# The first input projection as three rounded products, and the norms between products taken tile by tile

## The chip, the cores and the metric

The kernel runs on one core of one Trainium2 chip. The metric is the device time of one execution in microseconds. TensorE (PE) multiplies, and its weight loads are shown as an engine of their own (PEld). VectorE (DVE), ScalarE (ACT) and GpSimd (POOL) do the rest of the arithmetic, and SyncE (SP) issues the loads of the weights.

## The reference, cut to what matters

Two sequences of 256 tokens each, the latents and their context, of width 1024, go through a stack of layers. Every layer is a norm, a product with a weight matrix, a mixer of some kind (attention, mLSTM, RWKV, a gated feed-forward), and a product back that is added to the residual rows. All inputs and outputs are float32. What the change touches is this:

```
def rms_norm(x, eps=NORM_EPS):
    xf = x.astype(jnp.float32)
    return (xf * lax.rsqrt(jnp.mean(xf * xf, axis=-1, keepdims=True) + eps)).astype(x.dtype)

def modulate(x, shift, scale):
    return rms_norm(x) * (1.0 + scale) + shift

def ab_mixer(h_l, h_c, w_in, gate_b, q_norm, k_norm, ...):
    splits = [NA_WIDTH, 2 * NA_WIDTH, 3 * NA_WIDTH, 3 * NA_WIDTH + ML_WIDTH, ...]
    def project(h):
        qa, ka, va, qb, kb, vb, ob, g = jnp.split(h @ w_in, splits, axis=-1)
        qa = rms_norm(split_heads(qa, NA_HEADS, NA_HEAD_DIM)) * q_norm
        ka = rms_norm(split_heads(ka, NA_HEADS, NA_HEAD_DIM)) * k_norm
        ...
    qa_l, ka_l, va_l, qb_l, kb_l, vb_l, ob_l, g_l = project(h_l)
    qa_c, ka_c, va_c, qb_c, kb_c, vb_c, ob_c, g_c = project(h_c)
```

`w_in` is 1024 x 3600: seven parts of 512 columns and 16 columns of gates.

## The kernel before

Token rows lie in `x` (latents) and `cx` (context), each as two tiles of 128 tokens by 1024. A norm's result is wanted the other way round, as eight blocks of 128 features by 256 tokens, so every norm ends in 16 transposes on PE. Weights come in slabs of 1024 rows by 512 columns (2 MB) through a ring of three places. SP issues the load of a slab when PE has used the slab three before it.

There are two kinds of product. The first (`rows_pe`, line 557) multiplies float32 by float32. The profile records two matmuls for each one written, so the 224 matmuls of the first projection stand as 448. The second kind works with rounded parts (float32r): each operand is split into a rounded high part and a low part, which is what the rounding left, and three products high x high, high x low, low x high are summed (`rows3_pe` line 380, `mlp_pe` lines 1366 and 1381, the feed-forwards line 2249). There the high part of a slab is made by ACT (`high_act`, line 336, two halves of four blocks), the low part by DVE (`low_dve`, line 343), one or two slabs ahead of PE.

Each engine has its own program, written out in order at the end of `bidir_dual_stack`. Nothing is rearranged by a scheduler, so what stands behind a waiting instruction on its engine waits too. Semaphores tie the engines together through named events.

**The first projection.** `first_mod_dve` (line 532) applies scale and shift to the eight blocks `hT[:, k, :]` (512 tokens wide: latents and context together). `ab_in_pe` then runs seven slabs of four token tiles by eight blocks, in PSUM banks 0 to 3, and after that the four gate products of four columns each, `psum[0:4, 4 + g, :]` (line 763), each with all 512 tokens as moving operand. `ab_in_act` copies every finished tile out of PSUM (lines 776 to 782). `qk_norm_dve` takes squares of `qa` and `ka`, POOL the root, DVE multiplies (line 801), PE transposes (line 833), and DVE copies out of PSUM (line 812) before the neighbourhood attention starts (line 857). POOL meanwhile loads and masks the attention's bias table (`bias_pool`, line 633) ahead of these roots.

**The norms between products.** There are eleven places: L0m with C0m, L1a with C1a, L1m, pre0, mix0, xx0, post0, pre1, mix1, xx1, post1 (L: latents, C: context; the others latents). At each the chain is: DVE adds the product to the rows (line 2221, or 1340 and 1342 with a gate); when the last tile is added, ACT takes squares of both tiles (`norm_act`, line 408, 1024 wide); POOL makes the inverse root of both (`norm_pool`, lines 416 and 418); DVE multiplies both tiles (line 428, into `sc`); PE transposes, block by block and in it tile by tile (`norm_pe`, line 471), so nothing starts before tile 1 is there; DVE copies out. For a product in rounded parts that is, for each block, high and low: lines 449 and 452 without a shift, lines 441, 444 and 446 with one. Otherwise it is one instruction (lines 456, 458). The next product waits for pairs of blocks. In the DVE program the norm of L0m is done, then the low part of the next slab, then the norm of C0m, and only then does the first feed-forward (`mlp0`) start on PE:

```
            norm_pe(pe, "L0m")
            norm_pe(pe, "C0m")
            mlp_pe(pe, "mlp0", x_parts, (0, 1), "L0m")
```

## Time and profile before

| | |
|---|---|
| time, median of 3 runs | 3435.55 us (3427.95 to 3437.43) |
| the profiled execution | 3440.02 us, its span 3438.2 us, mean granted clock 0.941 |
| PE busy | 3122.3 us (91%) |
| PEld busy | 2324.8 us (68%) |
| DVE busy | 1697.6 us (49%) |
| ACT busy | 963.3 us (28%) |
| POOL busy | 282.4 us (8%) |
| read from HBM | 400.67 MB, 117 GB/s over the span |

Start and duration in a row of the timeline are microseconds from the span's start; "x16" counts instructions that were merged into the row, and the bracket gives idle time of the engine before it and what ended it. A matmul's recorded duration includes its way through the array, so successive matmuls overlap: the rate is read from the distance between starts.

### The profile page before, as it was taken

How to read it: one execution, taken by the hardware profiler on the slowest of the kernel's cores; microseconds unless marked ns; L12 is line 12 of the kernel's file. 1: busy time of each engine (PE TensorE's matmuls, PEld its weight loads, DVE VectorE, ACT ScalarE, POOL GpSimd, SP SyncE). 2: the span in 40 equal slices, each digit the busy share in tenths (PEclk: the TensorE clock that was granted, in tenths of full speed). 3: DMA queues.
4: the chain of work that ended last, by engine and by line, in shares of the span. 5: the costliest groups of instructions: out<-in, count | busy, mean ns of one | idle time of the engine just before them, and what ended most of it. 6: DMA issues, size and time to landing. Idle time of an engine off the chain costs nothing. (4 is left out here: it accounts for less than half of the span.)

```text
span 3438.2 us, 54550 instructions
## 1 busy us (share of the span) xinstructions
PE 3122.3 (91%) x24312; PEld 2324.8 (68%) x24312; DVE 1697.6 (49%) x2689; ACT 963.3 (28%) x1489; POOL 282.4 (8%) x362
## 2 busy tenths in 40 slices
PE   7999988799996977989978989999899999998899
PEld 2443333398994536888866979874579898455697
DVE  1104356465556108777755555455445453465453
ACT  1012310133331115443312333322223332142332
POOL 1202011000000012232310000000000000200000
PEclk9998989899998988999979999999999999999999
DMA  8311344245453210000024545542245554323253
GB/s 252 102 55 62 135 147 172 73 147 196 172 196 95 92 25 2 3 3 3 4 81 141 193 150 172 187 165 89 98 144 168 165 183 169 128 74 123 74 192 128
DMA packets 249827, 409.23 MB, mean 119 GB/s; under 512 B 10055, under 2 KB 102616, under 8 KB 249464
## 3 DMA queue, kind: packets, MB, share of 16 engines
q1 hardware_dynamic: 244824, 390.39, 33.3%
q0 software_dynamic: 4768, 15.35, 1.8%
q8 instruction: 191, 3.13, 0.4%
q14 instruction: 44, 0.36, 0.0%
HBM read 400.67 MB, written 2.95 MB: 117 GB/s over the span
## 5 line engine op out<-in xcount | busy, mean ns | idle before, releaser
L343 DVE TENSOR_TENSOR ring_parts<-ring,arena_parts 128x2048 fp32r<-128x2048 f32 x250 | 553.0, 2254 | 276.9 <-ACT arena_parts L336 274.6
L336 ACT CAST arena_parts<-ring 128x2048 fp32r<-128x2048 f32 x250 | 457.3, 1879 | 601.3 <-PE psum L2249 229.5
L2249 PE MATMUL psum<-arena_parts 128*128 128x256 f32 x2816 | 514.8, 286 | 6.4 <-DVE arena_parts L452 6.2
L2249 PEld LDWEIGHTS psum<-arena_parts 128*128 128x128 f32 x2816 | 444.0, 194 | 9.2 <-DVE arena_parts L452 9.2
L557 PE MATMUL psum<-ring,hT 128*128 128x512 f32 (+1 forms) x960 | 414.2, 593 | 9.1 <-DVE hT L1308 2.6
L2249 PE MATMUL psum<-arena_parts,ring_parts 128*128 128x256 f32 x1408 | 400.8, 285 | 0.0
L557 PEld LDWEIGHTS psum<-ring,hT 128*128 128x128 f32 x960 | 184.0, 192 | 234.5 <-issue 223.1
L380 PE MATMUL psum<-arena_parts 128*128 128x512 f32 x928 | 291.9, 396 | 8.3 <-DVE arena_parts L2285 8.1
L2249 PEld LDWEIGHTS psum<-arena_parts,ring_parts 128*128 128x128 f32 x1408 | 272.9, 194 | 0.0
L1381 PE MATMUL psum<-arena_parts 128*128 128x512 f32 x768 | 240.5, 395 | 7.8 <-DVE arena_parts L1428 7.8
L380 PEld LDWEIGHTS psum<-arena_parts 128*128 128x128 f32 x928 | 176.8, 191 | 46.6 <-DVE arena_parts L2285 9.0
L680 PE MATMUL psum<-ring,arena 128*24 128x512 f32 (+2 forms) x384 | 188.4, 625 | 3.1 <-DMA ring<-in_ada_w 3.1
L1366 PE MATMUL psum<-arena_parts 128*128 128x256 f32 x1024 | 187.9, 286 | 3.6 <-DVE arena_parts L446 3.6
L380 PE MATMUL psum<-ring_parts,arena_parts 128*128 128x512 f32 x464 | 182.6, 394 | 0.0
L1381 PEld LDWEIGHTS psum<-arena_parts 128*128 128x128 f32 x768 | 145.7, 191 | 38.5 <-DVE arena_parts L1428 8.4
L1366 PEld LDWEIGHTS psum<-arena_parts 128*128 128x128 f32 x1024 | 162.3, 195 | 5.1 <-DVE arena_parts L446 4.7
L1381 PE MATMUL psum<-ring_parts,arena_parts 128*128 128x512 f32 x384 | 151.3, 394 | 0.0
L1366 PE MATMUL psum<-arena_parts,ring_parts 128*128 128x256 f32 x512 | 146.0, 285 | 0.0
L2280 DVE TENSOR_TENSOR sc<-sc,psum 128x512 f32<-128x512 f32 x44 | 30.3, 688 | 228.5 <-PE psum L2249 228.5
L2731 PE MATMUL psum<-ring,hT 128*128 128x512 f32 x256 | 126.9, 626 | 1.3 <-DMA ring<-in_xmem_wkv 1.3
L416 POOL TENSOR_SCALAR stat<-stat 128x2 f32<-128x2 f32 x17 | 3.6, 210 | 1479.0 <-issue 1167.2
L471 PE MATMUL psum<-const,sc 128*128 128x128 f32 x240 | 52.9, 395 | 68.9 <-DVE sc L428 68.9
(407 smaller groups left out, 5095.4 us busy)
## 6 DMA issues: line engine op xcount, KB each, us to landing
ring<-in_mlp_w SPq DMA_DIRECT2D x48, 2048.0 KB, 7.8
ring<-in_ada_w SPq DMA_DIRECT2D x24, 2048.0 KB, 8.0
ring<-in_ffn_pre_w_gu SPq DMA_DIRECT2D x44, 1024.0 KB, 6.9
ring<-in_ffn_post_w_gu SPq DMA_DIRECT2D x44, 1024.0 KB, 7.1
ring<-in_ffn_pre_w_down SPq DMA_DIRECT2D x8, 2048.0 KB, 7.9
ring<-in_xmem_wkv SPq DMA_DIRECT2D x8, 2048.0 KB, 8.1
ring<-in_ffn_post_w_down SPq DMA_DIRECT2D x8, 2048.0 KB, 7.8
ring<-in_ab_w_in SPq DMA_DIRECT2D x7, 2048.0 KB, 8.3
```

The source lines that it names most:

```text
L336: nc.scalar.copy(high_view(name)[:, k, :], raw_view(name)[:, k, :]).then_inc(*up(act, ("high", name, h)))
L343: nc.vector.tensor_tensor(low_view(name)[:, k, :], raw_view(name)[:, k, :], high_view(name).bitcast(F32)[:, k, :], ALU.subtract)\
L380: ins = nc.tensor.matmul(psum[:, b, :], lhs[q][:, k0 + k, P * t:P * t + P], s[:, k, :], start=(k0 + k == 0 and i == 0), stop=(k0 + k == kt ...
L416: nc.gpsimd.tensor_scalar(s[:, 2:4], s[:, 0:2], 1.0 / D, EPS, ALU.mult, ALU.add).then_inc(*up(pool))
L471: ins = nc.tensor.transpose(psum[:, b + 4, at:at + 128], sc[:, 2 * t + k // 4, 128 * (k % 4):128 * (k % 4) + 128], ident)
L557: ins = nc.tensor.matmul(psum[:, where[t], 0:w], lhs(k0 + k, tile), s[:, k, 0:w], start=(k0 + k == 0), stop=(k0 + k == kt - 1))
L680: ins = nc.tensor.matmul(rows, csil[:, k, 22 - 2 * i:22 - 2 * i + 2 * ns], s[:, k, :], start=False, stop=(i == ns - 1 and k == KT - 1))
L1366: ins = nc.tensor.matmul(psum[:, b, 256 * j:256 * j + 256], s[:, k, at:at + P], src[q][:, k, :], start=(k == 0 and i == 0), stop=(k == 7 a ...
L1381: ins = nc.tensor.matmul(psum[:, b, :], hid_groups[g % 2][q][:, k, P * t:P * t + P], s[:, k, :], start=(g == 0 and k == 0 and i == 0), sto ...
L2249: ins = nc.tensor.matmul(psum[:, b, 256 * j:256 * j + 256], s[:, k, at:at + P], x_parts[q][:, k, :], start=(k == 0 and i == 0), stop=(k == ...
L2280: nc.vector.tensor_tensor(t, t, psum[:, 2 * (n % 2) + 1, :], ALU.mult)\
L2731: ins = nc.tensor.matmul(psum[:, 6 + i, :], hT[:, k, 256 + P * i:256 + P * i + P], s[:, k, :], start=(k == 0), stop=(k == KT - 1))
```

## The change

The first projection now works in rounded parts. The buffer `sc` gets a float32r view on the same bytes. For each slab half ACT makes the high part (`ab_high_act`, into `sc` for the first half, into the place of `so` for the second) and DVE the low part in the ring (`ab_low_dve`). The blocks of `hT` are split too, each when it has been modulated: high by ACT (`first_high_act`, into the place of `qaT` and `kaT`), low by DVE. A slab is multiplied in halves, block by block and in it tile by tile, with banks 0 to 3 and 4 to 7 by turns. The gate columns are put at columns 0, 32, 64 and 96 of a zeroed 128-column block, and one product of eight blocks (times three) gives all four gates in bank 4; it comes before the last slab (`AB_ORDER`). The squares of `qa` and `ka` and their multiplication are moved between the slab halves, ACT takes two of the eight copies behind the transposes, and the rope on POOL no longer waits for the gates.

The norms between products go by token tile and half: ACT takes squares of 512 columns when these are added (`squares_act`), POOL makes the root for each tile (`norm_rstd_pool`), DVE multiplies a tile in two halves right behind its last addition (`norm_tile_dve`, called from inside `gated_rows_dve` and `add_rows_dve`), and PE transposes tile 0 and then tile 1 (`norm_turn_pe`). Behind the transposes ACT makes the high part (`norm_out_act`) and DVE the low part (`norm_out_dve`); where there are no parts they take two blocks each in turn. The product waits for single blocks. C0m is transposed inside `mlp0`, behind its first slab. At xx0 and xx1 DVE does the norm before it copies the memory's keys out (`mem_turn_dve`).

```diff
         plan_ada(0, 0, 4)
-        plan_rows("ab_in", a["ab_w_in"][0], KT, 3600)
+        AB_ORDER = (0, 1, 2, 3, 4, 5, 7, 6)
+        for n in AB_ORDER:
+            plan(("ab_in", n, 0), a["ab_w_in"][0], KT, 512 * n, min(512, 3600 - 512 * n))
...
+        def squares_act(act, key, name, n, t):
+            stage(act, "norm")
+            act.wait_ge(*when((name, "added", n, t + 2 if key[0] == "C" else t)))
+            s = norm_stat(act, key)
+            nc.scalar.activation(sc[:, 4 + n, :], norm_tile(key, t)[:, 512 * n:512 * n + 512], ACT.Square,
+                                 scale=D ** -0.5, accum_out=s[:, 2 * t + n:2 * t + n + 1]).then_inc(*up(act, (key, "squares", n, t)))
+            act.wait_ge(*latest(act))
...
+        def norm_tile_dve(dve, key, t):
...
+            dve.wait_ge(*when((key, "rstd", t)))
+            for n in range(2):
+                c = slice(512 * n, 512 * n + 512)
+                nc.vector.tensor_scalar(norm_rows(key, t)[:, c], norm_tile(key, t)[:, c], s[:, 6 + t:7 + t], None,
+                                        ALU.mult).then_inc(*up(dve, (key, "normed", t) if n else (key, "half normed", t)))
+
+        def norm_turn_pe(pe, key):
+            stage(pe, "norm")
+            norm_stat(None, key)
+            for t in range(2):
+                rows = norm_rows(key, t)
+                for k in range(KT):
+                    pe.wait_ge(*when((key, "half normed" if k < 4 else "normed", t)))
...
+                    if t and k % 2:
+                        ins.then_inc(*up(pe, (key, "turned", k // 2)))
...
         def ab_in_pe(pe):
-            rows_pe(pe, "ab_in", lambda k, t: hT[:, k, P * t:P * t + P], range(4), KT, 3584, [0, 1, 2, 3], each="first")
             stage(pe, "ab")
-            s = slab(pe, ("ab_in", 7, 0))
-            for g in range(4):
-                pe.wait_ge(*bank(4 + g, ("gates", g)))
-                for k in range(KT):
-                    ins = nc.tensor.matmul(psum[0:4, 4 + g, :], s[:, k, 4 * g:4 * g + 4], hT[:, k, :],
-                                           start=(k == 0), stop=(k == 7))
...
+                    for k in range(4 * h, 4 * h + 4):
+                        if i == 0:
+                            pe.wait_ge(*when(("first", "low", k)))
+                        for t in range(4):
+                            b = t + 4 * ((i + 1) % 2)
+                            if k == 0:
+                                pe.wait_ge(*bank(b, ("ab_in", n, t)))
+                            tile = slice(P * t, P * t + P)
+                            for j, (w, y) in enumerate(((high, ab_high_x), (high, hT_parts), (low, ab_high_x))):
+                                ins = nc.tensor.matmul(psum[:, b, :], y[:, k, tile], w[:, k - 4 * h, :],
+                                                       start=(k == 0 and j == 0), stop=(k == 7 and j == 2))
...
         def ab_in_act(act):
...
+            for n in range(7):
+                if n == 5:
+                    ab_high_act(act, 7, 0)
+                if n < 6:
+                    ab_high_act(act, n + 1, 0)
+                if n == 6:
+                    gates_act(act)
+                ab_out_act(act, AB_ORDER.index(n))
+                if n < 6:
+                    ab_high_act(act, n + 1, 1)
...
                     nc.vector.tensor_tensor(dst, dst, tmp, ALU.add).then_inc(*up(dve, (name, "added", n, t)))
                     dve.wait_ge(*latest(dve))
+                    if n and t in norm:
+                        norm_tile_dve(dve, norm[t], t % 2)
...
                     also(("used", slab_at[w]), (name, "full", 2 * n + 1))
+                    if name == "mlp0" and n == 0:
+                        norm_turn_pe(pe, "C0m")
```

The order of work on ACT from the first copy behind the modulation to the first exponential of the attention, before (`L782`, `L778`, `L780`, `L776` copy finished tiles, `L1035` are the gates):

```order
L698 COPY adab<-psum 8x512
L782 COPY arena<-psum 128x512 x16
L778 ACTIVATE arena<-psum 128x512 x4
L780 COPY arena<-psum 128x4x128 x4
L776 ACT_TABLE_LOAD
L776 ACTIVATE arena<-psum 128x512 x4
L1035 ACTIVATE arena<-psum,stat 4x512 x2
L1035 ACTIVATE sc<-psum,stat 4x512 x2
L952 ACT_TABLE_LOAD
```

and the end of the same stretch in the changed kernel (`L907` high parts of slab halves, `L1261` the gates, `L969` the sigmoids of the last slab, `L1038` two of the copies behind the transposes):

```order
L907 CAST ring_parts<-ring 128x8x128
L907 CAST sc_parts<-ring 128x2048
L973 COPY arena<-psum 128x4x128 x4
L907 CAST arena_parts<-ring 128x2048
L1261 ACTIVATE arena<-psum,stat 4x512 x2
L1261 ACTIVATE sc<-psum,stat 4x512 x2
L969 ACT_TABLE_LOAD
L969 ACTIVATE arena<-psum 128x512 x4
L1038 ACTIVATE arena<-psum,colA 128x4x128 x2
L1177 ACT_TABLE_LOAD
```

The high part of a slab half now stands ahead of, and another behind, the copies of the slab before; the gates stand ahead of the last slab's sigmoids.

DVE around L0m and C0m, before (`L446` the last low block of L0m, `L343` the low part of `mlp0`'s first slab, `L428` the multiplication of both tiles of C0m):

```order
L441 TENSOR_SCALAR sc<-psum,stat,modcol 128x256
L444 CAST arena_parts<-sc 128x256
L446 TENSOR_TENSOR arena_parts<-sc,arena_parts 128x256
L343 TENSOR_TENSOR ring_parts<-ring,arena_parts 128x2048 x2
L428 TENSOR_SCALAR sc<-cx,stat 128x1024 x2
L431 TENSOR_SCALAR stat<-modcol 128x8
L441 TENSOR_SCALAR sc<-psum,stat,modcol 128x256
```

and in the changed kernel, from the second half of the additions on (`L1567` and `L1569` add, `L511` multiplies a half tile, `L576` and `L579` make a low block):

```order
L1567 TENSOR_TENSOR sc<-psum,arena 128x512
L1569 TENSOR_TENSOR x<-x,sc 128x512
L511 TENSOR_SCALAR sc<-x,stat 128x512 x2
L1567 TENSOR_TENSOR sc<-psum,arena 128x512
L1569 TENSOR_TENSOR cx<-cx,sc 128x512
L506 TENSOR_SCALAR stat<-modcol 128x8
L511 TENSOR_SCALAR arena<-cx,stat 128x512 x2
L1567 TENSOR_TENSOR sc<-psum,arena 128x512
L1569 TENSOR_TENSOR cx<-cx,sc 128x512
L576 TENSOR_SCALAR sc<-psum,stat,modcol 128x256
L579 TENSOR_TENSOR arena_parts<-sc,arena_parts 128x256
```

The multiplications moved in between the additions; the two low parts (`L343`) moved ahead of all eight additions of this product, and those of C0m behind the first outputs that `mlp0` needs.

## Rows read from the trace of the kernel before

**Rows 1.** The page's first part: busy time, share of span, instructions of each engine.
```profile
PE 3122.3 (91%) x24312; PEld 2324.8 (68%) x24312; DVE 1697.6 (49%) x2689; ACT 963.3 (28%) x1489; POOL 282.4 (8%) x362
```

**Rows 2.** Timeline of PE: the first projection, its gates, the first scores.
```profile
54.26 194.20 PE L557 MATMUL psum<-ring,hT 128*128 128x512 f32 x448 [2.26 <-DVE hT L532]
248.39 27.63 PE L763 MATMUL psum<-hT,ring 128*4 128x512 f32 x64
...
286.87 5.16 PE L857 MATMUL psum<-arena 64*128 64x512 f32 x6 [1.45 <-DVE arena L812]
```

**Rows 3.** Timeline of PE: products in rounded parts, 512 columns, in mlp0c.
```profile
1052.26 0.62 PE L1381 MATMUL psum<-arena_parts 128*128 128x512 f32 x2
...
1052.94 0.62 PE L1381 MATMUL psum<-arena_parts 128*128 128x512 f32 x2
```

**Rows 4.** The page's fifth part, costliest groups: low and high parts of slabs.
```profile
L343 DVE TENSOR_TENSOR ring_parts<-ring,arena_parts 128x2048 fp32r<-128x2048 f32 x250 | 553.0, 2254 | 276.9 <-ACT arena_parts L336 274.6
L336 ACT CAST arena_parts<-ring 128x2048 fp32r<-128x2048 f32 x250 | 457.3, 1879 | 601.3 <-PE psum L2249 229.5
```

**Rows 5.** Timelines of DVE and POOL in the first projection.
```profile
53.37 5.26 DVE L532 TENSOR_SCALAR hT<-hT,stat,modcol 128x256 f32<-128x256 f32 x16
...
93.04 9.06 POOL L633 TENSOR_TENSOR arena<-arena,const 128x4096 f32<-128x4096 f32 x1 [12.24 <-DMA arena<-bias_rows]
...
98.12 4.53 DVE L794 TENSOR_TENSOR sc<-arena 128x512 f32<-128x512 f32 x1 [4.01 <-ACT arena L782]
```

**Rows 6.** Windows of all engines: the span between projection and settled attention.
```profile
283.70:311.00 27.30, 23.34 (x49) 9.34 (x50) 13.36 (x27) 7.07 (x16) 18.09 (x39) 0.50 0.00 0
```

**Rows 7.** Timeline of the gap at post0, from the last addition on.
```profile
2511.83 0.69 DVE L2221 SCALAR_TENSOR_TENSOR x<-psum,x 128x512 f32<-128x512 f32 x1 [6.17 <-PE psum L557]
2512.56 1.06 ACT L408 ACTIVATE sc<-x 128x1024 f32<-128x1024 f32 x1 [24.95 <-DVE x L2221]
...
2516.11 1.54 DVE L428 TENSOR_SCALAR sc<-x,stat 128x1024 f32<-128x1024 f32 x2 [3.59 <-POOL stat L418]
...
2517.71 3.46 PE L471 MATMUL psum<-const,sc 128*128 128x128 f32 x15 [0.25 <-DVE sc L428]
...
2525.63 0.48 DVE L452 SCALAR_TENSOR_TENSOR arena_parts<-psum,colB,arena_parts 128x256 fp32r<-128x256 f32 x1
```

**Rows 8.** Windows of all engines: the transposes and outputs of that gap.
```profile
2517.00:2521.20 4.20, 3.93 (x18) 3.66 (x19) 3.03 (x7) 2.90 (x2) 0.00 (x0) 0.50 0.57 184
```

**Rows 9.** Timeline at mix0: ACT's copy of one 256-column block, DVE's run-ahead low part.
```profile
2226.13 4.50 DVE L343 TENSOR_TENSOR ring_parts<-ring,arena_parts 128x2048 fp32r<-128x2048 f32 x2 [7.45 <-ACT arena_parts L336]
...
2247.68 0.37 ACT L2358 COPY arena<-psum 128x256 f32<-128x256 f32 x1 [6.38 <-PE psum L2334]
```

**Rows 10.** Timeline of PE at L0m and C0m: last product, first product of mlp0.
```profile
654.52 16.04 PE L557 MATMUL psum<-ring,hT 128*128 128x512 f32 x37
...
693.57 0.48 PE L1366 MATMUL psum<-arena_parts 128*128 128x256 f32 x2
```

**Rows 11.** Timeline of DVE at L1a and C1a: last addition, first mixing instruction.
```profile
1061.37 0.69 DVE L1340 TENSOR_TENSOR sc<-psum,arena 128x512 f32<-128x512 f32 x1 [4.02 <-PE psum L1381]
...
1075.05 4.39 DVE L1536 TENSOR_TENSOR arena<-hT 128x4064 f32<-128x4064 f32 x1
```

**Rows 12.** Timeline of DVE at L1m: last addition, end of the outputs.
```profile
1828.89 0.69 DVE L1340 TENSOR_TENSOR sc<-psum,arena 128x512 f32<-128x512 f32 x1 [5.45 <-PE psum L557]
...
1846.09 0.43 DVE L446 TENSOR_TENSOR arena_parts<-sc,arena_parts 128x256 fp32r<-128x256 f32 x1
```

**Rows 13.** Timeline at mix1: last addition, first product of mla_in.
```profile
2919.21 0.69 DVE L2221 SCALAR_TENSOR_TENSOR x<-psum,x 128x512 f32<-128x512 f32 x1 [3.39 <-PE psum L380]
...
2929.83 10.54 PE L557 MATMUL psum<-ring,hT 128*128 128x512 f32 x24 [1.28 <-DVE hT L456]
```

**Rows 14.** Timelines of DVE and PE at xx0: last addition, first product of xq0.
```profile
2419.89 0.69 DVE L2221 SCALAR_TENSOR_TENSOR x<-psum,x 128x512 f32<-128x512 f32 x1 [6.18 <-PE psum L557]
...
2428.81 1.20 PE L380 MATMUL psum<-arena_parts 128*128 128x512 f32 x2
```

More of the change, by code:

```diff
@@ L473, in norm_pe, with plus_column, norm_form @@
                 ins.then_inc(*up(pe, (key, "turned", b)))
+        PLUS = {"L0m": (0, 0, 3), "C0m": (0, 1, 3), "L1a": (1, 0, 0), "C1a": (1, 1, 0), "L1m": (1, 0, 3)}
+        GAINS = {"pre": "ffn_pre", "mix": "mix", "xx": "xmem", "post": "ffn_post"}
+        def plus_column(key):
+            return stat[:, 8:16] if key[0] == "L" else stat[:, 16:24]
+        def norm_form(key):
+            if key in PLUS:
+                layer, v, i = PLUS[key]
+                return plus_column(key), mcol(layer, v, i), {"L0m": x_parts, "L1m": x_parts, "C0m": c_parts}.get(key)
+            dest = {"mix1": None, "xx0": q_parts, "xx1": q_parts}.get(key, x_parts)
+            return gain(GAINS[key[:-1]], int(key[-1])), None, dest
@@ new lines, in norm_out_act @@
+        def norm_out_act(act, key):
+            stage(act, "norm")
+            scale, shift, dest = norm_form(key)
+            off = 256 if key[0] == "C" else 0
+            if key in PLUS:
+                act.wait_ge(*when((key, "scale")))
+            for k in range(KT):
+                b = k // 2
+                if dest is None and b % 2 == 0:
+                    continue
+                act.wait_ge(*when((key, "turned", b)))
+                src_ = psum[:, norm_bank(key, b), 256 * (k % 2):256 * (k % 2) + 256]
+                to = hT[:, k, off:off + 256] if dest is None else dest[0][:, k, :]
+                if shift is None:
+                    ins = nc.scalar.activation(to, src_, ACT.Copy, scale=scale[:, k:k + 1])
+                else:
+                    ins = nc.scalar.activation(to, src_, ACT.Identity, bias=shift[:, k:k + 1], scale=scale[:, k:k + 1])
+                if dest is not None:
+                    ins.then_inc(*up(act, (key, "high", k)))
+                else:
+                    ins.then_inc(*up(act, ((key, "part"), k)))
+                    if k % 2:
+                        also(("read", (key, b)), ((key, "part"), k))
@@ L1531, in mix_dve @@
         def mix_dve(dve):
-            dve.wait_ge(*latest(dve))
+            for key in ("L1a", "C1a"):
+                for k in range(KT):
+                    dve.wait_ge(*when(((key, "part"), k)))
             stage(dve, "mix")
@@ L2222, in add_rows_dve @@
                     also(("read", (name, n, i)), (name, "added", n, i))
+                    if n and norm is not None:
+                        norm_tile_dve(dve, norm, i)
+                        stage(dve, "add")
                 if n == 0:
@@ L2329, in even_in_pe @@
                     for k in range(KT):
-                        pe.wait_ge(*when(("read", ("mix0", k // 2))))
+                        pe.wait_ge(*when((("mix0", "part"), k)))
                         if k % 4 == 0:
@@ L2568, in mla_pe @@
             rows_pe(pe, "mla_in", lambda k, t: hT[:, k, P * t:P * t + P], range(2), KT, 800, [0, 1],
-                    [("read", ("mix1", b)) for b in range(4)], only=(0,))
+                    only=(0,), each=("mix1", "part"))
             norm_pe(pe, "xm1")
@@ L2960, in _ @@
             high_ahead(act, "mem0")
-            norm_act(act, "xx0", x, [("sbg_out", "added", 1, 1)])
+            for n in range(2):
+                for t in range(2):
+                    squares_act(act, "xx0", "sbg_out", n, t)
+            norm_out_act(act, "xx0")
             xq_act(act, 0)
@@ L2975, in _ @@
             high_ahead(act, "mem1")
-            norm_act(act, "xx1", x, [("mla_out", "added", 1, 1)])
+            for n in range(2):
+                for t in range(2):
+                    squares_act(act, "xx1", "mla_out", n, t)
+            norm_out_act(act, "xx1")
             xq_act(act, 1)
@@ L2979, in _ @@
             high_ahead(act, "post1")
[L2980 removed]
+            for n in range(2):
+                for t in range(2):
+                    squares_act(act, "post1", "xo1", n, t)
+            norm_out_act(act, "post1")
             swiglu_act(act, "post1")
@@ L3091, in _ @@
             readout_pool(pool)
-            norm_pool(pool, "L1m")
+            for t in range(2):
+                norm_rstd_pool(pool, "L1m", t)
             mem_load(pool)
```

468 lines of the change are left out of this document (326 added, 142 removed).

## The prediction

> **What bounds the kernel now.** I read the engine shares first: PE is busy for 91% of the span, and the next engine, DVE, for 49% [rows 1]. So time comes back in two ways only: fewer or shorter matmuls, or fewer stretches in which PE waits. The change does one of each. Next I read PE's timeline in the first projection. It stands without an idle stretch from 54.26 to the last gate product at 276.02 [rows 2], and its speed is its own: no wait lies inside. Last I read the places between two products. At post0 the last addition starts at 2511.83, PE's transposes run from 2517.71 on, and the last low block is ready at 2526.11 [rows 7]. What ends each wait there is the chain of addition, squares, root, multiplication, transposes and outputs, one after another. The granted clock in that stretch was 0.50, the lower of its two levels, 1.2 GHz [rows 8].
>
> All sums are made against the profiled execution, 3440.02 us, which lies 4.5 us above the median of 3435.55; I take that off at the end.
>
> **The projection.** Before, 224 written products in float32 take 194.20 us, 0.867 each, and 32 gate products 27.63, 0.863 each [rows 2]. In rounded parts, three products with 512 columns start within 1052.94 - 1052.26 = 0.68 us, 0.227 each [rows 3]. The changed kernel has 7 slabs x 32 x 3 = 672 products of this size, and 8 x 3 = 24 for the gates, together 696 x 0.227 = 157.8 us. Before it is 276.0 - 54.3 = 221.7. The gates alone shrink from 27.6 to 5.4, since four thin products cost as much as four full ones each time, and one padded one replaces them. Against this: the modulation takes 5.26 / 8 = 0.66 per block [rows 5], and now two blocks of it and a low part of about 0.7 stand ahead of the first product, where one block stood, so it starts 1.15 us later (part of the 1.35 lay ahead of 54.26 already); and I add 2 us for products at the low clock at the start. Sum: 221.7 - 157.8 - 1.15 - 2 = **60.9 less**.
>
> The price beside PE is the splitting. A half slab costs ACT 1.88 and DVE 2.25 [rows 4]; PE works 32 / 2 x 3 x 0.227 = 10.9 us on one. Per slab of 21.8 us ACT has 2 x 1.88 and four copies (some 2.3 together), 6.1 in all; DVE has 4.5, and in the first slabs the squares of qa and ka. High and low of the next half come one after another, 4.1 us, inside the 10.9 that PE spends on the other half, so I cost them at nothing. If that cover failed for all 14 halves, it would be 14 x 4.1 = 57 us. The split of slab 0 needs only the slab and free engines and lies before 54. The new padding for the gates stands ahead of the split on DVE, but the gates' slab is needed half a slab and more behind that.
>
> One collision is in the trace. DVE's square at 98.12 took 4.53 us, where its like takes 0.69, and ended when POOL's masking of the bias, 93.04 to 102.10, ended [rows 5]. In the changed kernel DVE's low part of the third slab falls there, and is wanted by PE at about 100.4. If it is held until 102.1 and then goes on, PE waits 2 to 4 us; if not, nothing. The Trainium skill ("SBUF — State Buffer", on who interferes with whom) says that a VectorE instruction with two SBUF inputs and a GpSimd one exclude each other; by that the whole 2 to 4 us would come, and the trace agrees in this one row. I take 1, inside the 3 us of allowance below, since the overlap hangs on a microsecond of timing.
>
> A page also bears on the rate: the Trainium skill ("FP8 and Floating Point Precision", notes on TensorE precision) gives true float32 four passes, so three rounded passes would be 0.867 x 0.75 = 0.65 us, and the projection some 7 us less still. The row says 0.68, and I go by the row.
>
> **Between projection and attention.** Before, PE's last gate product ends at 276.02 and the first score starts at 286.87, 10.9 us, in which DVE copies and multiplies qa and ka in turn [rows 2]. Now the multiplication is done during the projection, and ACT takes two of the eight copies. What is left behind the last slab: about a microsecond of transposes and six DVE copies, or, on ACT, a table load, four sigmoids and two copies of 0.6 each. The latter is 1.3 + 2.4 + 1.2 = 4.9 with the load as an estimate, hence 5.2: **5.7 less**.
>
> **The norms.** T is the end of the last product, e the end of the last addition, T + 0.72. Before, at post0: from e to DVE's multiplication 3.59 (two squares passes of 1.06 with 0.12 between, then 1.2 for POOL), 1.54 for the multiplication, transposes 3.46, and then DVE's two outputs of each block; the last is ready at 2526.11 = T + 14.3 [rows 7]. After: only the last tile's second half is left when the last addition ends. Squares of 512 columns are half of 1.06 and the read, 0.75; POOL 1.2; half the multiplication 0.45; the first four transposes of tile 1 at 3.46 / 15 = 0.23. So the first pair of blocks stands at e + 3.1. ACT then makes a high block in 0.37 (its copy of the same shape [rows 9]), eight by e + 6.1, and DVE's last low block follows at e + 7.1 = T + 7.8. That is 6.5 less. The same chain with what each place has of its own:
> - post0 and post1: 6.5 each, 13.0.
> - mix0 and pre1: DVE does the low part of a slab ahead of the additions (4.50 for two at 2226.13 [rows 9]) and ends it late, and now also waits for tile 0's root ahead of tile 1's last addition. I take 1.75 off: 4.75 each, 9.5.
> - xx0 and xx1: before, the first product starts 8.9 behind the last addition's start [rows 14], and DVE feeds a block in 0.9 where PE uses one in 0.68, so the stream starts in effect at T + 9.5. After, the first block is ready at T + 5.2: 4.4 each, 8.8.
> - mix1: 2919.21 to 2929.83 is 10.6 [rows 13]; after, the first block stands at T + 4.3: 6.3.
> - pre0: the wait for tile 0's root holds the last gated addition by 2.6 of the 6.5: 3.9.
> - L1m: 1828.86 to 1846.52 is 17.7 [rows 12]; DVE's two instructions a block are 0.92 together and bound the end, T + 12.9: 4.8.
> - L1a with C1a: 1061.34 to 1075.05 is 13.7 [rows 11], after T + 6.95: 6.8.
> - L0m with C0m: the last product ends at 670.56, `mlp0` starts at 693.57, 23.0 behind [rows 10]. After, C0m is out of the way; the additions run to T + 1.55, eight blocks of 0.92 end at T + 8.9, and PE uses a block in 0.36, so it starts in effect at T + 6.4. The transposes of C0m, 1.9, come back inside `mlp0`: 23.0 - 6.4 - 1.9 = 14.7. DVE's and ACT's outputs of C0m (7.4 and 3.0) lie beside PE's work there.
>
> Sum: 13.0 + 9.5 + 8.8 + 6.3 + 3.9 + 4.8 + 6.8 + 14.7 = **67.8 less**. Where a wait on a root is added, what is queued behind it on DVE is the addition of tile 1, and behind that ACT's squares; that is what the 1.75 and the 2.6 are for.
>
> **The clock.** Streams behind a gap begin at 0.50 now [rows 8], and shorter gaps don't make it worse than that; yet where a gap loses its transposes at that level, the same cold start may fall on products. I allow **3 more**, bounds 0 and 12 (eleven places at about 1.1).
>
> Total: -60.9 - 5.7 - 67.8 + 3 = -131.4, thus 3308.6 for an execution like the profiled one and 3304 for the median.
>
> **The rivals.**
> - Norms give half. If DVE's waits on roots, or ACT at 0.47 a block rather than 0.37, or cold products lie behind each gap, 20 to 34 us of the 67.8 stay away: 3323 to 3338. For it: DVE is the engine that bounds the outputs before, and every new wait stands in its row. Against: the chain's pieces are from rows of the same shapes. Chance 0.17.
> - The attention's first part runs faster. From 283.7 to 311.0 PE is busy for 23.3 us at 0.50 [rows 6]. If a shorter gap before it keeps the clock up, about 10 us go: 3294. Chance 0.10.
> - The splitting shows. ACT or DVE is late at every half slab: 57 us come back, 3361. Against: 4.1 stands against 10.9. Chance 0.05.
> - More gain, from the rate or gaps that close wholly: 3275 to 3289. Chance 0.05.
> - Slower than before. PE's clock stays at 0.50 through the whole projection and on into the attention: at half the rate 696 products take 696 x 0.43 = 297 us rather than 221.7 (estimated from rows at the higher level, less what does not scale), and the scores behind it lose as much as they work; some 3500. It decides once nearly all of the projection, over 97% of it, is at the lower level. Against: the rounded products of rows 3 run at the pitch of the upper one. Chance 0.01.
> - The change doesn't do what it says (three products as slow as two of float32): projection unchanged, 3365, in the 0.05 of the splitting.
>
> **The numbers.** The forecast, 3304, has its own range of 3289 to 3319 with 0.62. Taking in the fast attention and the norms at half, 3284 to 3336 leaves out less than 2 in 10. A measurement of this kernel tells some 0.3%, 10 us, from no change; every case but the clock's lies over 70 us below, so: faster 0.98, same 0.01, slower 0.01.
>
> **What would show it.** Starts of products 0.68 us apart by threes in the projection without waits from the second slab on; gates of 5.4 us; first score near 221 us, 5 behind the last product; a gap at post0 of 8 us to its last low block in place of 14.3; no wait at C0m; additions of tile 1 held at pre0 and mix0 by at most 3 us. The forecast fails if PE waits for a low part at slab after slab, if the norm gaps stay over 10 us, or if the product pitch in the projection is above 0.23.

## The result

The changed kernel takes 3303.66 us (median of 4 runs, 3302.96 to 3308.48), the kernel before 3436.49 (3427.95 to 3439.34). The ratio is 0.962, its 95% interval 0.9601 to 0.964. The forecast was 3304, within 3284 to 3336. The profiled execution of the changed kernel took 3304.0 us with a span of 3302.2, 136.0 less than that of before; the sum had said 131.4 less. So the hit of the median is closer than the sum behind it, and the parts below show which errors met.

The page's first part after, against [rows 1]:

```profile
PE 3038.7 (92%) x24496; PEld 2349.9 (71%) x24496; DVE 1695.1 (51%) x2652; ACT 1040.9 (32%) x1658; POOL 293.9 (9%) x391
```

PE is as dense as before and has 84 us less to do. PE's timeline at the start and at the end of the projection, against [rows 2]:

```profile
51.28 0.41 PE L837 MATMUL psum<-const,adab 8*128 8x8 f32 x4 [0.66 <-ACT adab L826]
55.31 0.77 PE L950 MATMUL psum<-sc_parts,arena_parts 128*128 128x512 f32 x1 [3.61 <-issue]
55.87 0.63 PE L950 MATMUL psum<-sc_parts,hT_parts 128*128 128x512 f32 x1
...
219.68 4.07 PE L1058 MATMUL psum<-const,arena 128*128 128x128 f32 x32
224.83 1.95 PE L1082 MATMUL psum<-arena 64*128 64x512 f32 x4 [1.07 <-ACT arena L1038]
```

The projection starts at 55.31 rather than 54.26 (forecast 1.15 later, measured 1.05) and ends at 219.7 rather than 276.0. It gained 56.3, not 60.9; the products of the gates took 5.8 (191.90 to 197.65) rather than 5.4. The first score starts at 224.83, 5.15 behind it rather than 10.9: 5.8 gained, forecast 5.7. PE waits nowhere between the slabs. ACT and DVE within a slab, their timelines:

```profile
100.84 2.67 ACT L975 COPY arena<-psum 128x512 f32<-128x512 f32 x4 [7.05 <-PE psum L950]
103.40 1.91 ACT L907 CAST arena_parts<-ring 128x2048 fp32r<-128x2048 f32 x1
114.18 1.90 ACT L907 CAST sc_parts<-ring 128x2048 fp32r<-128x2048 f32 x1 [8.87 <-PE psum L950]
```

```profile
116.11 2.29 DVE L912 TENSOR_TENSOR ring_parts<-ring,sc_parts 128x2048 fp32r<-128x2048 f32 x1 [8.48 <-ACT sc_parts L907]
```

ACT stands idle for 7 to 9 us of each half until PE is done. The low part of 116.11 is ready at 118.40, 6.6 us before PE starts on it at 125.02. The cover that the prediction named is there, and the 57 us of exposed splitting didn't come.

The gap at post0 after, all engines, against [rows 7]:

```profile
2405.84 1.38 PE L524 MATMUL psum<-const,sc 128*128 128x128 f32 x8
...
2406.04 0.69 DVE L2460 SCALAR_TENSOR_TENSOR x<-psum,x 128x512 f32<-128x512 f32 x1 [3.30 <-PE psum L684]
2406.82 0.63 ACT L485 ACTIVATE sc<-x 128x512 f32<-128x512 f32 x1 [6.14 <-DVE x L2460]
...
2408.10 0.56 POOL L497 TENSOR_TENSOR stat<-stat,half 128x1 f32<-128x1 f32 x1
2408.70 0.88 DVE L511 TENSOR_SCALAR sc<-x,stat 128x512 f32<-128x512 f32 x2 [1.97 <-POOL stat L497]
2409.24 1.53 PE L524 MATMUL psum<-const,sc 128*128 128x128 f32 x8 [2.02 <-DVE sc L511]
2409.77 3.03 ACT L543 ACTIVATE arena_parts<-psum,colB 128x256 fp32r<-128x256 f32 x8 [2.23 <-PE psum L524]
2410.73 3.23 DVE L571 SCALAR_TENSOR_TENSOR arena_parts<-psum,colB,arena_parts 128x256 fp32r<-128x256 f32 x8 [1.15 <-ACT arena_parts L543]
```

From the end of the last addition, 2406.73, DVE's multiplication starts 1.97 later (forecast 1.95), ACT's high blocks end at 2412.80 (e + 6.1, forecast 6.1) and the last low block at 2413.96 (e + 7.2, forecast 7.1). That is the chain as it was priced.

### The profile page after: what moved, and what is told of

Read it like the earlier page. It is cut to its first block and busy times, and to the rows that moved or that the text cites. A ratio compares the mean times of both kernels' runs of the same rounds, so it can differ in the third digit from the quotient of the medians.

```text
span 3302.2 us, 55139 instructions
## 1 busy us (share of the span) xinstructions
PE 3038.7 (92%) x24496; PEld 2349.9 (71%) x24496; DVE 1695.1 (51%) x2652; ACT 1040.9 (32%) x1658; POOL 293.9 (9%) x391
## 5 line engine op out<-in xcount | busy, mean ns | idle before, releaser
L684 PE MATMUL psum<-ring,hT 128*128 128x512 f32 (+1 forms) x512 | 221.2, 593 | 5.6 <-DVE hT L1535 2.6
L684 PEld LDWEIGHTS psum<-ring,hT 128*128 128x128 f32 x512 | 99.0, 195 | 123.5 <-issue 114.3
L494 POOL TENSOR_SCALAR stat<-stat 128x1 f32<-128x1 f32 x26 | 8.1, 311 | 1416.1 <-ACT sc L485 1416.1
L2156 PE MATMUL psum<-ring,hT 64*64 64x64 f32 x2560 | 108.3, 236 | 4.8 <-DVE ring L2179 3.5
```

Source lines behind the costliest of these rows:

```text
L684: ins = nc.tensor.matmul(psum[:, where[t], 0:w], lhs(k0 + k, tile), s[:, k, 0:w], start=(k0 + k == 0), stop=(k0 + k == kt - 1))
L2156: ins = nc.tensor.matmul(psum[h, b, 64 * c:64 * c + 64], B[left][z][h, c, :], B[right][z][h, c, :], start=True, stop=True)
```

## Place by place

Both programs have the same products between the norms, so I read at each place the time from the start of the last product ahead of it to the start of the 97th matmul behind the transposes, 96 behind the first, in both traces (at L1a to the first; at L0m up to the last product ahead of L1a). This takes in the cold start of the stream.

| place | before | after | gained | forecast |
|---|---|---|---|---|
| L0m, C0m (to L1a) | 390.9 | 376.5 | 14.4 | 14.7 |
| L1a, C1a | 28.95 | 22.02 | 6.9 | 6.8 |
| L1m | 29.53 | 23.73 | 5.8 | 4.8 |
| pre0 | 24.97 | 21.76 | 3.2 | 3.9 |
| mix0 | 24.20 | 20.39 | 3.8 | 4.75 |
| xx0 | 39.54 | 35.01 | 4.5 | 4.4 |
| post0 | 25.93 | 18.30 | 7.6 | 6.5 |
| pre1 | 24.21 | 20.39 | 3.8 | 4.75 |
| mix1 | 44.21 | 37.59 | 6.6 | 6.3 |
| xx1 | 39.53 | 36.62 | 2.9 | 4.4 |
| post1 | 25.92 | 19.91 | 6.0 | 6.5 |

They sum to 65.5, where 67.8 was forecast. The clock has its share in them. At xx0 and xx1 the first product comes 4.20 us behind in both, but at xx1 PE's clock was at 0.50 for 8.4 us of the stretch and at xx0 for 5.3. At post0 four of the kernels below (tiles outermost, products ahead of the projection, C0m ahead, POOL twice) have the same instructions and took 19.8 rather than 18.30, with 6.8 us at 0.50 rather than 3.4.

The rest of the 136.0 is 62.0 up to the first score, 6.5 between it and L0m, and 2.0 scattered over the stretches between. The 6.5 were not in the sum. PE's clock was at 0.50 for 27.3 us behind the projection before [rows 6]; after, the windows view gives (columns: stretch, its length, busy us of PE, PEld, DVE, ACT, POOL, the granted clock, DMA share, GB/s):

```profile
54.60:61.40 6.80, 6.09 (x14) 4.84 (x15) 6.80 (x17) 3.52 (x6) 0.00 (x0) 0.50 1.03 260
61.40:100.00 38.60, 38.60 (x168) 31.23 (x167) 9.36 (x12) 8.68 (x9) 8.88 (x5) 1.00 0.80 178
228.60:242.30 13.70, 12.26 (x25) 4.55 (x26) 5.71 (x13) 3.59 (x9) 11.82 (x25) 0.50 0.01 1
```

The low stretch is 13.7 us long, and once the program is past both low stretches, 4.1 of the 6.5 us are gained. Over the whole execution the low stretches sum to 334.7 us, before to 408.8.

## The experiments

The kernel before was measured again beside each group of experiments: 3432.09 us beside the first four, 3433.76 beside the next four, 3432.51 beside the last four, against 3436.49 beside the changed kernel. So a difference between a median here and the changed kernel's 3303.66 is uncertain by 3 to 4 us, and the places in the traces decide.

**One part of the change alone.** Two kernels, each with one half of the diff.

> The kernel before with the first projection's part of the change alone (rounded products, the gates' padded product, qk's squares and multiplication between the slabs); the norms are as before. If the time is a sum of the two parts, the trace of the changed kernel gives 56.3 us at the last product of the projection, 5.8 behind it and some 6.5 in the attention and the mLSTM from shorter stretches at the low clock: 68.6 less than before, about 3368. If the 6.5 us behind the first score came with the norms or by chance, only 62 less, 3374. If the parts hinder each other, more than 72 less.

> The kernel before with the norms' part of the change alone; the first projection is float32 as before. Theory of the sum: 67.4 less, about 3369, with the same gap at each place as in the changed kernel (post0: last low block 8.1 us behind the last product). Rival: some of the 67.4 hangs on the projection (its buffers, the clock), then 50 to 60 less.

The projection alone takes 3367.68 us (3363.06 to 3370.23; ratio 0.9809, interval 0.9794 to 0.9823), the norms alone 3372.23 (3370.43 to 3375.62; 0.9825, 0.981 to 0.9839), beside 3432.09 of before. The sum of the two gains, 64.4 and 59.9, is 124.3, against 132.8 for the whole change by medians. By these medians alone the rivals would stand: 64.4 lies between 62 and 68.6, and 59.9 in the range of 50 to 60. The traces decide against them. Their spans are 69.8 and 68.3 us shorter than before, 138.1 together against 136.0 for both parts. With the projection alone the last product ahead of L0m starts at 600.5 (670.0 before, 601.4 with both), and from there to the end the time is the same as before, 2768.0 and 2768.3. With the norms alone each place has the value of the table within 0.3 us, but for xx1, where it is 35.30. So the parts neither help nor hinder each other by more than the few us that these measurements tell. The clock's gain goes with the projection, as the windows of the two kernels show:

```profile
227.50:241.10 13.60, 11.84 (x25) 4.05 (x24) 6.57 (x15) 4.41 (x11) 11.68 (x25) 0.50 0.00 1
```

```profile
280.10:304.00 23.90, 18.90 (x43) 7.85 (x42) 14.30 (x27) 5.58 (x12) 20.61 (x43) 0.50 0.12 45
```

The first is the projection alone, the second the norms alone, whose low stretch of 23.9 us is near the 27.3 of before.

**Why the products are 0.232 apart.** The forecast had 0.227, from the feed-forward. In the changed kernel 96 products of a slab take 22.29 us, 0.2322 each:

```profile
102.72 0.40 PE L950 MATMUL psum<-sc_parts,arena_parts 128*128 128x512 f32 x1
...
125.02 0.40 PE L950 MATMUL psum<-sc_parts,arena_parts 128*128 128x512 f32 x1
```

Over 672 this is 3.5 us, most of the 4.6 by which the projection fell short. The gates have 0.4 of it, and the first slab 0.8: it took 2.8 us longer than the others, where 2 were forecast.

```diff
-                    for k in range(4 * h, 4 * h + 4):
-                        for t in range(4):
+                    order = [(k, t) for k in ks for t in ts] if i == 0 else [(k, t) for t in ts for k in ks]
+                    for k, t in order:
```

> The changed kernel, but from the second slab on the projection's half slab is multiplied token tile by token tile and in it block by block, so twelve products in a row go to one PSUM bank rather than three. Products of the projection start 0.2322 us apart in the changed kernel, 0.2267 in the feed-forward, where 24 in a row go to one bank. If the changing bank costs the difference, the distance falls to 0.227 to 0.228 and the time by 2.5 to 3.3 us. If it is where the operands lie, or which weights follow which, it stays at 0.231 to 0.233 and the time within 0.5 us.

The distance stayed at 0.2322 from slab to slab, and the time within scatter (3306.59, 3299.72 to 3308.53). The bank is not it. (Over rows of 96 the feed-forward's distance is 0.2270; 0.2267 is a third of 0.68.) The groups of instructions by line for 102 to 216 us (mean ns behind the busy time) show where the matmuls are longer, in the changed kernel:

```profile
L950 PE MATMUL psum<-ring_parts,arena_parts 128*128 128x512 f32 x157 | 61.5, 392 | 0.0
L950 PE MATMUL psum<-sc_parts,hT_parts 128*128 128x512 f32 x80 | 31.8, 398 | 0.0
...
L950 PE MATMUL psum<-arena_parts 128*128 128x512 f32 x76 | 30.2, 397 | 0.0
```

So I moved what lies in the arena, by an edit of seven numbers, of which three are:

```diff
-        so = area(12304, 4, 512)
+        so = area(12352, 4, 512)
-        ab_high_x = area(14352, KT, 512, rounded=True)
+        ab_high_x = area(14400, KT, 512, rounded=True)
-        nab = area(18448, 2, 4, 8, 64)
+        nab = area(18496, 2, 4, 8, 64)
```

> The changed kernel with the second half slab's high part, the high parts of hT, and what else lies there (so, qaT, kaT, the bias) 48 words further on in the arena. Twelve products in a row to one bank left the distance of the projection's products at 0.232, so the bank is out. Matmuls whose moving operand lies in sc or at 12304 of the arena last 398 ns by the trace, the feed-forward's (highs at 15360) 389. If the place in the arena counts, the distance in the second halves (now 0.2311) falls towards 0.2267 while the first halves, whose high part is in sc, keep most of 0.2333. If not, both stay within 0.0005.

The shift leaves some other use of that memory where it was, so part of what follows is computed from other values; the instructions and their sizes are those of the changed kernel. The second halves' products are now 0.2271 apart (0.2311), the first halves', of whose operands only the high parts of `hT` have moved, 0.2324 (0.2334), and the projection's last product starts at 217.5 rather than 219.5. The group's mean shows it:

```profile
L950 PE MATMUL psum<-arena_parts 128*128 128x512 f32 x78 | 30.4, 390 | 0.0
```

So where the operands lie changes the rate, and in the second halves it accounts for the whole difference from the feed-forward. It isn't all: in the changed kernel the first half of the last slab has its high part in `sc` like the six before it and ran at 0.2311, which no run explains. 12304 words are no multiple of 64, 12352 are; whether that is the rule, or how the operands lie to each other, these runs don't tell, and the first halves, whose high part is in sc, were not tried elsewhere. The median, 3304.81, doesn't show 2 us.

**POOL's long instruction.**

> The changed kernel with POOL's addition of the window mask done twice (the second adds the mask once more, which the output does not depend on in its digits or does in masked places alone). In the changed kernel POOL's one lies from 95.49 to 105.04 and DVE's low part at 105.34 takes 2.29. If a DVE instruction with two operands in SBUF is held for as long as POOL's runs, the low part of 105.34 ends near 114 to 117 rather than 107.6, and PE waits up to 3 us for it at about 113.9. If they share, it takes at most 5 us and PE doesn't wait.

DVE and PE in this kernel, with POOL's second instruction ahead of them:

```profile
105.30 9.08 POOL L767 TENSOR_TENSOR arena<-arena,const 128x4096 f32<-128x4096 f32 x1
```

```profile
105.50 11.03 DVE L915 TENSOR_TENSOR ring_parts<-ring,arena_parts 128x2048 fp32r<-128x2048 f32 x1 [9.23 <-ACT arena_parts L910]
```

```profile
116.59 0.79 PE L953 MATMUL psum<-arena_parts 128*128 128x512 f32 x1 [2.34 <-DVE ring_parts L915]
```

The low part starts 0.2 behind POOL, is held until POOL ends at 114.38, and ends at 116.53; PE waits 2.34 us. The median, of two runs, is 3307.99. In the changed kernel's own trace the order was the other way: DVE began at 93.82, POOL at 95.49, and POOL's took 9.55. Which of them comes first is decided by a microsecond. In the kernel of the next experiment DVE came second:

```profile
93.90 10.49 DVE L912 TENSOR_TENSOR ring_parts<-ring,sc_parts 128x2048 fp32r<-128x2048 f32 x1 [8.48 <-ACT sc_parts L907]
```

and PE waited 1.47 us at 104.44; with the tiles outermost it was 11.20 and 2.18. The prediction had 2 to 4 us for this wait if it came. In the two traces in which it came by itself it is 1.5 and 2.2, and in the changed kernel's own it didn't come. The Trainium skill ("SBUF — State Buffer", on who interferes with whom) has it as a lock between such instructions; all four traces agree.

**The wait for tile 0's root.**

```diff
-                    if n and norm is not None:
-                        norm_tile_dve(dve, norm, i)
+                    if n and i and norm is not None:
+                        norm_tile_dve(dve, norm, 0)
+                        norm_tile_dve(dve, norm, 1)
```

> The changed kernel, but at L1m, pre0 and all places of the second half DVE adds tile 1 before it multiplies tile 0 of the norm, so that addition no longer waits for tile 0's root. In the changed kernel the last addition starts 2.5 us behind the last product's end at pre0 and 1.7 at mix0 and pre1 (forecast 2.6 and 1.75). If that wait is on the path, 5.5 to 7 us less than the changed kernel, all at these three places, and nothing elsewhere. Rival: tile 0's transposes and multiplication now lie behind the last addition and take the wait's place, 0.9 us more at each of ten places: up to 5 us more in all.

Measured: 3291.79 us (3288.9 to 3295.85), 11.9 less than the changed kernel's median; the gain over the kernel before of the same group is 140.3, 7.5 more than the changed kernel's 132.8, and the span is 8.1 shorter. In the changed kernel, DVE at pre0:

```profile
1933.90 0.69 DVE L1569 TENSOR_TENSOR x<-x,sc 128x512 f32<-128x512 f32 x1
...
1936.65 0.88 DVE L511 TENSOR_SCALAR sc<-x,stat 128x512 f32<-128x512 f32 x2 [2.06 <-POOL stat L497]
...
1937.44 0.68 DVE L1567 TENSOR_TENSOR sc<-psum,arena 128x512 f32<-128x512 f32 x1
```

and in this one:

```profile
1937.26 0.69 DVE L1567 TENSOR_TENSOR sc<-psum,arena 128x512 f32<-128x512 f32 x1 [0.23 <-PE psum L1619]
1937.99 0.69 DVE L1569 TENSOR_TENSOR x<-x,sc 128x512 f32<-128x512 f32 x1
...
1939.61 0.91 DVE L511 TENSOR_SCALAR sc<-x,stat 128x512 f32<-128x512 f32 x2 [0.93 <-POOL stat L497]
```

The addition no longer waits for POOL. By the measure of the table pre0 is at 20.41 (1.35 less), mix0 and pre1 at 17.49 (2.9 less each): 7.2, as expected. The first product comes 2.4 us earlier at pre0 and 1.9 at mix0 and pre1, so the waits themselves are near the forecast's 2.6 and 1.75; the rest of the 2.9 is the clock, whose 6.8 us at 0.50 at mix0 and pre1 are gone, while pre0 keeps its 6.8. Beyond it post1 fell by 2.2 and post0 by 0.6, where the first product comes no earlier, mix1 rose by 0.4, and from the first score to L0m it took 2.7 less, with 6.8 us at 0.50 rather than 13.7. At post0 and post1 the clock stayed up; at post1, the changed kernel and then this one:

```profile
3102.60:3109.40 6.80, 6.03 (x30) 5.64 (x28) 5.32 (x9) 6.78 (x11) 0.00 (x0) 0.50 0.54 175
```

```profile
3098.00:3104.80 6.80, 5.87 (x48) 5.63 (x47) 5.07 (x9) 6.75 (x11) 0.00 (x0) 1.00 0.58 186
```

So "nothing elsewhere" was wrong, by the clock.

**The clock, tried directly.**

```diff
+            for _ in range(n):
+                nc.tensor.matmul(psum[:, b, 0:128], ident, ident, start=True, stop=True)
```

> The changed kernel with eight float32 products of 128 columns that nothing reads, in the gap between the transposes of tile 0 and tile 1, at eight places (L0m, L1a, L1m, pre0, mix0, post0, pre1, mix1, post1 without the two of the memory). PE idles there for 2.0 to 2.8 us. Theory of the clock: kept busy, PE's clock does not fall behind the gap, where the first products now run at 0.50 for 3 to 7 us; 1 to 2 us less at each, 8 to 16 in all. Rival: they run at the lower level themselves, 3.5 rather than 1.8 us, hold the transposes up by 1 to 1.5 us each, and the clock falls as before: 8 to 14 us more.

> The changed kernel with twelve such products in the 3.6 us in which PE waits before the projection, and with two of the ada products moved into the wait behind the second score of the attention. In the changed kernel the clock is at 0.50 from 54.6 to 61.4 and from 228.6 to 242.3. If what counts is how busy PE was before, the first stretch goes or is cut, 2 to 3 us less, and the second is cut by half, 2 to 3 us less. Rival: the clock falls anyway, and the time stays within 1 us or rises by what the idle products overrun, 1 us.

The edit puts the products in nine gaps, not eight. In the gaps the first theory held for the clock at four of them, and for the time in part. At mix0, post0, pre1 and post1 the low stretch is gone, and the places gained 1.2, 0.6, 1.2 and 2.2 us, not 1 to 2 at each of all. (The same four lost their low stretch in the kernel with tile 1's addition first, without such products.) At L0m the idle products delayed the stream (first product 5.8 rather than 4.0 behind), 2.5 lost by the 97th matmul and 3.9 up to L1a; and behind L1a, 1.6 later, the clock fell in a stretch where it had not, here with the changed kernel's beside it:

```profile
1032.00:1046.80 14.80, 14.80 (x29) 6.33 (x29) 3.51 (x6) 1.75 (x3) 0.00 (x0) 0.54 0.35 134
```

```profile
1023.90:1035.30 11.40, 10.88 (x37) 4.94 (x34) 5.39 (x8) 2.13 (x4) 0.00 (x0) 1.00 0.55 189
```

PE was busy throughout the first, and lost some 7 us. But the products in the gaps are not shown to be the cause. With the norms alone, a kernel that has none of them, the clock fell in the same stretch, and PE was as busy:

```profile
1096.00:1109.60 13.60, 13.60 (x27) 7.50 (x27) 0.00 (x0) 1.64 (x3) 0.00 (x0) 0.50 0.08 31
```

In the shifted kernel and in the one with the high part on DVE it fell there for 6.8 us. The total is 3310.73 (3309.36 to 3312.81), 7 more. What made the clock fall there, the runs don't tell.

Ahead of the projection it worked: with twelve products in the wait of 4.03 us, which they fill without lengthening it, the first slab's products were 0.2321 apart (0.2617 in the changed kernel), 2.8 us less. Without them the clock is at 0.50 for 3.4 us in six traces with the rounded projection and for 6.8 in four, the changed kernel's among them; the first slab then takes 1.3 to 1.6 or 2.6 to 2.8 us more than with them, so that is the gain. In the attention the stretch at 0.50 came in two pieces of 6.8 and 3.4 rather than 13.7, and came back at 307 for 6.8; from the first score to L0m it took 377.6 us against 376.6. The moved ada products are not shown to do anything: four kernels without them had 6.8 to 10.2 there. The total, 3302.0 (3299.45 to 3304.04), is 1.7 less, within scatter.

**C0m back ahead of the feed-forward.**

> The changed kernel with C0m's transposes and outputs put back ahead of the first feed-forward. By the prediction's terms: DVE ends L0m's outputs at T + 8.9, multiplies C0m's last tile, and PE transposes it, so the first product starts at about T + 11.3 with all blocks there, in effect 4.9 later than in the changed kernel, less the 1.9 of transposes that no longer stand inside: 3 us more, with DVE's outputs of C0m (7.4) up to 3 more where the hidden units then wait for DVE. Rival: the place of C0m is worth nothing, since the low clock at the stream's start is spent in the wait: within 1 us.

PE's timeline:

```profile
602.93 1.91 PE L524 MATMUL psum<-const,sc 128*128 128x128 f32 x16
607.49 0.41 PE L524 MATMUL psum<-const,arena 128*128 128x128 f32 x2 [2.65 <-DVE arena_parts L579]
...
612.88 2.39 PE L524 MATMUL psum<-const,arena 128*128 128x128 f32 x10 [1.14 <-DVE arena_parts L579]
614.93 0.78 PE L1596 MATMUL psum<-arena_parts 128*128 128x256 f32 x2
```

C0m's transposes wait for banks that L0m's low parts free, and the first product starts 11.8 behind the last one's end rather than 3.4. From L0m to L1a it costs 3.6 us (380.1 against 376.5), the forecast 3 and a little. The median, 3310.64, is 7.0 higher and the span 4.6 longer; the place explains 3.6 of it.

**The high part on ACT or DVE.**

> The changed kernel, but at the seven places without a shift that want parts (pre0, mix0, xx0, post0, pre1, xx1, post1) DVE makes the high block too, as before the change. By the prediction's chain a block then costs DVE 0.91 rather than ACT 0.37 and DVE 0.40 side by side, so the last low block comes 3.2 later where PE is ready for it: 16 at the five feed-forwards and mixers, about 1 at xx0 and xx1, some 15 to 17 us more than the changed kernel. Rival: products at the low clock are slower than the feed anyway, so no more than half of that, 5 to 9.

3324.24 us (3321.02 to 3329.85), 20.6 more. Place by place: pre0 3.8, mix0 2.9, xx0 1.1, post0 3.8, pre1 2.9, xx1 0.1, post1 2.4, in all 17.0. DVE's alternation at mix0, one block each 0.91 us:

```profile
2149.47 0.48 DVE L573 TENSOR_SCALAR arena_parts<-psum,colB 128x256 fp32r<-128x256 f32 x1 [0.46 <-PE psum L524]
...
2149.99 0.48 DVE L576 SCALAR_TENSOR_TENSOR arena_parts<-psum,colB,arena_parts 128x256 fp32r<-128x256 f32 x1
2150.39 0.47 DVE L573 TENSOR_SCALAR arena_parts<-psum,colB 128x256 fp32r<-128x256 f32 x1
```

The rival, that cold products hide a slower feed, falls. The clock is part of the 17.0: at mix0, post0, pre1 and post1 it was at 0.50 for 10.2 us rather than for 6.8 (3.4 at post0). Of the norms' gain about a quarter is this move alone.

**A faster kernel.**

> The kernel with tile 1's addition ahead of tile 0's multiplication, and POOL's window mask in four instructions of 2.3 us rather than one of 9.06. In two traces DVE's low part met the long one and took 10.5 and 11.2 us, and PE waited 1.5 and 2.2. If POOL and DVE take turns by whole instructions, the low part is held by at most 2.3 or 4 in pieces, which PE's half slab hides: no wait of PE in the projection, 1 to 2 us less than the same kernel without the split (3291.8). Rival: DVE loses every turn and waits for all four: as before.

> The same with eight float32 products of 128 columns that nothing reads in the 4 us in which PE waits for the first block. With twelve of them the first slab's products were 0.2321 apart rather than 0.26, and the clock did not fall between 54 and 62. If eight do the same, 1.3 to 2.8 us less than without them; if eight are too few to hold the clock, within 1 us.

The split is inconclusive: in its trace POOL began behind DVE's low part (94.35 and 93.71), so the two never met in the way that costs, and 3291.16 (3289.92 to 3296.43) is 3291.79 again. With eight products ahead of the projection it is 3287.86 (3284.71 to 3289.98), ratio 0.9578 of before, interval 0.9563 to 0.9592. The windows of the first and the second kernel:

```profile
54.40:61.20 6.80, 5.93 (x14) 4.70 (x15) 6.76 (x17) 3.50 (x7) 0.00 (x0) 0.51 1.03 274
```

```profile
54.40:61.20 6.80, 6.00 (x26) 4.94 (x27) 6.80 (x16) 3.53 (x6) 0.00 (x0) 1.00 1.05 272
```

The projection's last product starts 2.8 earlier (216.5 and 219.3), as expected. It is the fastest kernel here, 15.8 under the changed one by medians, 11.8 if each is set against the kernel before that was measured beside it.

## Why the prediction came out

- **The projection, 60.9 forecast, 56.3 measured.** The count of products, the start and the hidden splitting were right. Mis-sized was the duration of a product, 0.227 from [rows 3]: it is 0.2322 in the projection, 3.5 us, and a part of that goes with where the operands lie. The prediction had named a pitch above 0.23 as a sign that it fails. By that sign it failed here, and the total still held, since 0.005 us a product is only 3.5 us. The 2 us for the cold start were 2.8, and the gates took 0.4 more. The Trainium skill's four passes for float32 ("FP8 and Floating Point Precision", notes on TensorE precision) had led to an estimate of 0.65 for three rounded products; the row's 0.68 was nearer to the 0.70 measured.
- **Behind it, 5.7 forecast, 5.8 measured.** It is ACT's path, as named: the table load 1.28, four sigmoids 2.06 and two copies 1.27, where 1.3, 2.4 and 1.2 were forecast.
- **The norms, 67.8 forecast, 65.5 measured.** The chain of post0 came out link by link. Taking the wait for a root at 2.6 and 1.75 was right: with tile 1 first the first product comes 2.4 and 1.9 earlier. The places are less exact than their sum. Above the forecast are post0 (7.6 rather than 6.5) and L1m (5.8 rather than 4.8), below it mix0 and pre1 (3.8 rather than 4.75), pre0 (3.2 rather than 3.9) and xx1 (2.9 rather than 4.4), and these partly cancel. At xx1 it is the clock: with the norms alone the same place had 4.0 us at 0.50 rather than 8.4 and gained 4.2.
- **The clock, +3 forecast (1 of it for POOL and DVE).** This term had the wrong sign. Outside the places of the table and the projection 8.5 us were gained, 6.5 of them ahead of L0m, and low stretches fell from 408.8 to 334.7 us in all. The rival of the faster start of the attention, at a chance of 0.10 and 10 us, came true at 4.1 by the end of the low stretch and 6.5 up to L0m.
- **The median.** 131.4 was forecast and 136.0 measured between the two profiled executions: the projection and the norms gave 4.6 and 2.3 less, and the clock's term was off by 11.5 the other way. That the profiled execution before lay 4.5 above its median, and the one after on it, made the median agree to 0.4 us. That is chance.
- **Slips that move nothing.** 221.7 - 157.8 - 1.15 - 2 is 60.75, not 60.9, and 696 x 0.43 is 299, not 297.
- **Not there:** splitting exposed, norms at half, a slower kernel. No wait of PE stands around C0m's transposes.

Open are what lowers the clock behind L1a and the rule for the operands' places. One stretch wanders: from L1a's first product to L1m the same instructions took 738 us before and after, and 735 to 746 in the other traces. It goes with the clock. In the traces of 735 us it was at 0.50 for 136 to 137 us of the stretch, in those before and after for 143 to 144, in the two of 743 and 746 for 154 to 155. That alone is as large as the effects of several experiments, and their medians should be read with it.

## What to carry to other kernels

Price a chain of small steps link by link from rows of the same shape: it held to a few tenths. Move the one long wait of an in-order engine behind the work that others wait for (7.2 us at three places here, for a few lines), and give two engines one output each rather than one engine both. Take a matmul's rate from operands in the same places, or allow 2% for it (0.2322 against 0.2270 here). Before you lay a change of a few us to an edit, look in the other traces whether the clock moved there without it.

## What the runs showed of the hardware

- Rounded products of 512 columns started 0.2270, 0.2311 or 0.2334 us apart at a granted clock of 1.00, with nothing waiting. Moving their operands by 48 words in SBUF changed 0.2311 to 0.2271.
- A POOL instruction of 9.06 us on SBUF and a DVE instruction with two SBUF operands exclude each other: DVE's 2.29 became 10.49, 11.03 and 11.20 when it came second, POOL's 9.06 became 9.55 and 11.04 when it did.
- In both kernels that filled PE's wait of 4 us ahead of the projection with float32 products that nothing reads, the granted clock stayed at 1.00 behind it; in the ten others with the rounded projection it was at 0.50 for 3.4 or 6.8 us.
- The granted clock fell to 0.50 in a stretch in which PE was busy throughout, for 13.6 us with the norms alone; in the same instructions of the changed kernel it stayed at 1.00.
